# Two feed-forward layers of a fused float32 model: the high weight parts meet 512 activation columns instead of twice 256

## The reference, cut to what matters

```python
def swiglu(h, w_gu, w_down):
    g, u = jnp.split(h @ w_gu, 2, axis=-1)
    return (jax.nn.silu(g) * u) @ w_down
h = h + swiglu(rms_norm(h, f_norm[layer]), f_w_gu[layer], f_w_down[layer])
```

## Time and profile before

| | |
|---|---|
| Median of 3 runs | 966.72 us (965.94 to 967.09) |
| Span of the profiled execution | 967.0 us |
| Instructions | 19359, of them 7852 matmuls |
| TensorE matmul busy | 952.0 us, 98% |
| VectorE busy | 712.7 us, 74% |
| ScalarE busy | 489.3 us, 51% |
| GpSimd busy | 86.6 us, 9% |
| Mean DMA rate | 193 GB/s |

### The profile page before, as it was taken

One profiled execution on the slowest core, in us unless ns is written; L12 is line 12 of the kernel. 1 busy time (PEld: TensorE's weight loads), 2 busy tenths in 40 slices (PEclk: granted clock), 3 DMA queues, 4 the chain that ended last, 5 costly groups with the idle time before them and its releaser, 6 DMA issues.

```text
span 967.0 us, 19359 instructions
## 1 busy us (share of the span) xinstructions
PE 952.0 (98%) x7852; PEld 918.1 (95%) x7852; DVE 712.7 (74%) x1135; ACT 489.3 (51%) x717; POOL 86.6 (9%) x132
## 2 busy tenths in 40 slices
PE   8999999999999999899999999999999999999998
PEld 8999999999999888589999999999999999999998
DVE  5896877777759878968777777699876676565654
ACT  6344744433447547847344434447667555433441
POOL 6000000000000042420000000020000000000000
PEclk9999999999999999999999999999999999999999
DMA  8756768686845762037586868436344357564621
GB/s 273 264 175 220 259 197 294 232 295 197 289 149 163 238 218 88 1 132 261 182 291 227 293 221 286 152 105 199 99 166 159 109 170 259 176 218 133 234 67 44
DMA packets 129836, 186.99 MB, mean 193 GB/s; under 512 B 6384, under 2 KB 100976, under 8 KB 129776
## 3 DMA queue, kind: packets, MB, share of 16 engines
q1 hardware_dynamic: 122000, 159.69, 50.2%
q0 software_dynamic: 6912, 25.17, 7.4%
q10 hardware_dynamic: 864, 1.29, 0.4%
HBM read 185.09 MB, written 1.05 MB: 192 GB/s over the span
## 4 chain that ended last, share of the span: by engine, by line
PE 89%; DVE 4%; ACT 3%; DMA 2%; issue 1%; SPq 1%; DVEq 0%; ACTq 0%
PE ps L1909 46%; PE ps L1987 19%; PE ps L1905 13%; PE ps L1907 4%; DMA g_raw<-in_a_w_in 2%; ACT g_hi L679 1%; PE ps L2117 1%; PE ps L2064 1%; PE ps L2182 1%; PE ps L2197 1%; DVE g_lo L1186 0%; ACT opb_hi L697 0%; SPq L522 0%; ACT e_odd L893 0%; PE ps L2309 0%
## 5 line engine op out<-in xcount | busy, mean ns | idle before, releaser
L1909 PE MATMUL ps<-opa_hi,g_hi 128*128 128x256 f32 x864 | 228.7, 286 | 0.7 <-ACT g_hi L679 0.4
L1909 PE MATMUL ps<-opa_lo,g_hi 128*128 128x256 f32 x864 | 220.7, 283 | 0.0
L1909 PE MATMUL ps<-opa_hi,g_lo 128*128 128x256 f32 x864 | 181.4, 283 | 0.0
L1304 DVE TENSOR_TENSOR g_lo<-g_raw,g_hi 128x2048 fp32r<-128x2048 f32 x54 | 123.8, 2293 | 69.0 <-ACT g_hi L753 69.0
L1909 PEld LDWEIGHTS ps<-opa_hi,g_hi 128*128 128x128 f32 x864 | 165.4, 191 | 4.0 <-issue 2.9
L1909 PEld LDWEIGHTS ps<-opa_lo,g_hi 128*128 128x128 f32 x864 | 162.3, 192 | 0.1
L1987 PE MATMUL ps<-hid_hi,d_hi 128*128 128x256 f32 x528 | 147.6, 279 | 0.1
L1987 PE MATMUL ps<-hid_hi,d_lo 128*128 128x256 f32 x528 | 147.5, 279 | 0.0
L1987 PE MATMUL ps<-hid_lo,d_hi 128*128 128x256 f32 x528 | 147.3, 279 | 0.0
L1186 DVE TENSOR_TENSOR g_lo<-g_raw,g_hi 128x2048 fp32r<-128x2048 f32 x54 | 123.6, 2290 | 31.7 <-ACT g_hi L679 28.7
L1909 PEld LDWEIGHTS ps<-opa_hi,g_lo 128*128 128x128 f32 x864 | 138.7, 192 | 0.0
(11 more groups left out here) (339 smaller groups left out, 1811.0 us busy)
## 6 DMA issues: line engine op xcount, KB each, us to landing
g_raw<-in_f_w_gu SPq DMA_DIRECT2D x44, 1024.0 KB, 8.8
ada_raw<-in_w_ada POOLq DMA_DIRECT2D x48, 512.0 KB, 6.2
d_raw<-in_f_w_down SPq DMA_DIRECT2D x22, 1024.0 KB, 5.2
g_raw<-in_w_in SPq DMA_DIRECT2D x14, 1024.0 KB, 8.3
g_raw<-in_w_gate SPq DMA_DIRECT2D x11, 1024.0 KB, 7.3
g_raw<-in_w_up SPq DMA_DIRECT2D x11, 1024.0 KB, 9.8
d_raw<-in_w_down SPq DMA_DIRECT2D x11, 1024.0 KB, 5.2
g_raw<-in_a_w_in SPq DMA_DIRECT2D x8, 1024.0 KB, 7.6
```

The source lines that it names most:

```text
L1304: dve.tensor_tensor(part_view(g_lo, g0 + r, True), raw_cols(c % 2, r % 2, True), part_view(g_hi, g0 + r, True).bitcast(F32), ALU.subtract) ...
L1909: mm = pe.matmul(pair(b)[:, a, :], wt[:, a * P:(a + 1) * P], xt, **st)
```

## The change

The two activation buffers `opa_hi`, `opa_lo` become the two halves of one buffer `opa` of 512 columns, and so do `opb_hi`, `opb_lo`. In layers 0 and 1, from step g0+1 on, one matmul of 512 columns takes the place of the two that share the high weights. Its left 256 columns (high activations) fall where the low-weight product is added too, its right 256 columns (low activations) fall into the right half of the same bank; the two halves are added afterwards: ScalarE copies the right halves to `gu`, VectorE adds the left halves to them, and the multiplication by `rstd` now reads `gu`. A step has two whole banks, two pairs of banks in turn. Step g0 keeps matmuls of 256 columns but lays its sums out in the same way. In ScalarE's order the Silu moves behind `g_hi`; in VectorE's order the two operations of the side sum move apart, one behind the multiplication by `rstd`, one behind `g_lo`. Layer 2 keeps its code.

```diff
-    opa_hi = sb("opa_hi", [P, KT, T], F32R)
-    opa_lo = sb("opa_lo", [P, KT, T], F32R)
+    opa = sb("opa", [P, KT, 2 * T], F32R)
+    opa_hi, opa_lo = opa[:, :, 0:T], opa[:, :, T:2 * T]
...
+                if f < 2:
+                    act.wait_ge(g_done, s4 + (g0 + r + 1))
+                    if not first or d0 + r >= 2:
+                        act.wait_ge(hid_lo_made, s4 + (d0 + r - 1))
+                    act.activation(gu[:, r % 2, :, :], gate_and_up(r)[:, :, T:2 * T], ACT.Copy).then_inc(cross_copied, 1)
                 else:
+                    silu()
...
                     act.activation(part_view(g_hi, g0 + r, True), raw_cols(c % 2, r % 2, True),
                                    ACT.Copy).then_inc(g_hi_made, 1)
+                if f < 2:
+                    silu()
...
-                product = gate_and_up(r)[:, :, 0:T] if f == 2 else pair(gbank(g0 + r))
+                product = gate_and_up(r)[:, :, 0:T]
+                if f < 2:
+                    dve.wait_ge(cross_copied, s4 + (d0 + r + 1))
+                    dve.tensor_tensor(gu[:, r % 2, :, :], product, gu[:, r % 2, :, :], ALU.add).then_inc(gu_summed, 1)
+                    dve.wait_ge(gu_summed, s4 + (d0 + r + 1))
+                    product = gu[:, r % 2, :, :]
...
+        def opening_step(g, x, hi_ready, ready):
+            pe.wait_ge(g_hi_made, g + 1)
+            pe.wait_ge(g_lo_made, g + 1)
+            pe.wait_ge(g_evac, evacs(g - 3))
+            for k in range(KT):
+                hi_ready(k)
+                product(g, g_hi, x, k, HI_COLS, start=(k == 0))
+                product(g, g_lo, x, k, HI_COLS)
+            for k in range(KT):
+                ready(k)
+                mm = product(g, g_hi, x, k, LO_COLS)
+            mm.then_inc(g_done, 1)
+
+        def wide_step(g, x, n):
+            pe.wait_ge(g_hi_made, n)
+            pe.wait_ge(g_lo_made, n)
+            for k in range(KT):
+                product(g, g_hi, x, k, BOTH_COLS, start=(k == 0))
+                mm = product(g, g_lo, x, k, HI_COLS)
+            mm.then_inc(g_done, 1)
...
-            g_step(g0, hi, lo, ready, hi_ready=hi_ready)
             if f == 2:
+                g_step(g0, xin_hi, xin_lo, ready, hi_ready=hi_ready)
                 sum_squares(norm)
-            g_step(g0 + 1, hi, lo, no_wait, late_lo=True)
-            if f < 2:
+                g_step(g0 + 1, xin_hi, xin_lo, no_wait, late_lo=True)
+            else:
+                opening_step(g0, x, hi_ready, ready)
+                pe.wait_ge(g_evac, evacs(g0 - 1))
+                wide_step(g0 + 1, x, g0 + 2)
                 sum_squares(norm)
...
-                elif s is None or s >= 2:
-                    pe.wait_ge(hid_made, i * 4 + (d0 + r - 1))
+                    g_step(g0 + r + 2, xin_hi, xin_lo, no_wait, waited=True)
                 else:
-                    g_free(g0 + s + 2 - 4)
-                g_step(g0 + r + 2, hi, lo, no_wait, waited=True)
+                    pe.wait_ge(gu_summed, i * 4 + (d0 + r + 1))
+                    wide_step(g0 + r + 2, x, i * 4 + (g0 + r + 3))
                 d_step(i, r, s)
```

More of the change, by code:

```diff
@@ L203, in layer_kernel @@
     over_b = ExitStack()
-    opb_hi = sb("opb_hi", [P, KT, T], F32R, on=over_b)
-    opb_lo = sb("opb_lo", [P, KT, T], F32R, on=over_b)
+    opb = sb("opb", [P, KT, 2 * T], F32R, on=over_b)
+    opb_hi, opb_lo = opb[:, :, 0:T], opb[:, :, T:2 * T]
     d_raw = sb("d_raw", [P, 2, 2, D], on=over_b)
@@ L281, in layer_kernel @@
     c_copied = sem("c_copied")
+    cross_copied, gu_summed = sem("cross_copied"), sem("gu_summed")
     gu_made, gate_scaled, k_copied, r_turned = sem("gu_made"), sem("gate_scaled"), sem("k_copied"), sem("r_turned")
@@ L377, in gate_and_up @@
         return ps[:, 4 + 2 * (g % 2):6 + 2 * (g % 2), :]
+    HI_COLS, LO_COLS, BOTH_COLS = slice(0, T), slice(T, 2 * T), slice(0, 2 * T)
     def kv_tiles(s):
@@ L743, in step, with silu @@
                 g = gu[:, r % 2, 0, :]
-                act.wait_ge(gu_made, s4 + (d0 + r + 1))
+                def silu():
+                    act.wait_ge(gu_made, s4 + (d0 + r + 1))
+                    if f < 2:
+                        act.activation(g, g, ACT.Silu).then_inc(silu_made, 1)
+                    else:
+                        act.activation(g, g, ACT.Silu, bias=shift_cols(r % 2)[:, 0:1]).then_inc(silu_made, 1)
                 if f < 2:
-                    act.activation(g, g, ACT.Silu).then_inc(silu_made, 1)
+                    act.wait_ge(g_done, s4 + (g0 + r + 1))
+                    if not first or d0 + r >= 2:
+                        act.wait_ge(hid_lo_made, s4 + (d0 + r - 1))
+                    act.activation(gu[:, r % 2, :, :], gate_and_up(r)[:, :, T:2 * T], ACT.Copy).then_inc(cross_copied, 1)
                 else:
-                    act.activation(g, g, ACT.Silu, bias=shift_cols(r % 2)[:, 0:1]).then_inc(silu_made, 1)
+                    silu()
                 if not tail and not ahead:
@@ L1251, in split_d, with ada_pair @@
                               ALU.subtract).then_inc(d_lo_made, 1)
-        def ada_pair(f, i, q):
+        def ada_pair(f, i, q, parts=(0, 1)):
             m0 = 24 * f + q
-            dve.wait_ge(ada_loaded[q % 2], i * 32 + 16 * (m0 // 2 + 1))
             acc = ada_acc[:, bass.ds(i * 512 + 3072 * f, 512)]
-            for half in range(2):
+            for half in parts:
+                if half == 0:
+                    dve.wait_ge(ada_loaded[q % 2], i * 32 + 16 * (m0 // 2 + 1))
                 k, raw = 2 * q + half, ada_raw[:, q % 2, half, :]
@@ L1290, in step @@
                     dve.tensor_copy(shift_cols(r % 2).unsqueeze(2), gate_and_up(r)[:, :, T:T + 1])
-                product = gate_and_up(r)[:, :, 0:T] if f == 2 else pair(gbank(g0 + r))
+                product = gate_and_up(r)[:, :, 0:T]
[4 more added lines that the diff above has]
+                    product = gu[:, r % 2, :, :]
                 dve.tensor_tensor(gu[:, r % 2, :, :], product,
                                   rstd[:, :].unsqueeze(1).to_broadcast([P, 2, T]), ALU.mult).then_inc(gu_made, 1)
+                with_ada = f < 2 and not tail and not ahead
+                if with_ada:
+                    ada_pair(f, i, r, (0,))
                 dve.wait_ge(gu_made, s4 + (d0 + r + 1))
@@ L1305, in step @@
                                       part_view(g_hi, g0 + r, True).bitcast(F32), ALU.subtract).then_inc(g_lo_made, 1)
+                if with_ada:
+                    ada_pair(f, i, r, (1,))
                 dve.wait_ge(hid_hi_made, s4 + (d0 + r + 1))
@@ L1317, in step @@
                     split_g(g0 + 3)
-                if f < 2:
-                    if not tail and not ahead:
-                        ada_pair(f, i, r)
             split_g(g0 + 2)
@@ L1911, in g_step, with product @@
                 mm.then_inc(g_done, 1)
+        def product(g, parts, x, k, cols, start=False):
+            for a in range(2):
+                mm = pe.matmul(gate_and_up(g)[:, a, cols], parts[:, g % 2, k, a * P:(a + 1) * P], x[:, k, cols],
+                               start=start, stop=(k == KT - 1), skip_group_check=True)
+            return mm
+        def opening_step(g, x, hi_ready, ready):
[17 more added lines that the diff above has]
+            mm.then_inc(g_done, 1)
         def g_free(g):
@@ L1916, in g_free @@
                 if first <= g < first + FT:
-                    pe.wait_ge(hid_made, FT * f + g - first + 1)
+                    pe.wait_ge(gu_summed, FT * (f + 1))
                     return
@@ L2053, in _ @@
         if last_stage >= 2:
-            ffn(0, 1, opa_hi, opa_lo, a_filled("n1"), a_hi_filled("n1"))
+            ffn(0, 1, opa, a_filled("n1"), a_hi_filled("n1"))
         if last_stage >= 3:
```

12 lines of the change are left out of this document (6 added, 6 removed).

## The result

The changed kernel takes 974.36 us (median of 4 runs, 973.45 to 976.26), the kernel before 966.33 us in the same comparison. The ratio is 1.0083, with a 95% interval of 1.0069 to 1.0098: **8.0 us slower**. Forecast were 971.9 us, in a range of 962 to 981.

A forecast was written before the change was run, and what follows sets the result against it. TensorE, with matmuls under way for 98% of the span, was taken as the bound. Terms +10.2 (waits), +3.0 (clock), +0.6 (layer ends), -0.6 (given back), -8.0 (wide matmuls) gave +5.2: 966.7 to 971.9 us, range 962 to 981.

The forecast's parts named there:

- The large term: Start of layers 0 and 1: g0+2 reuses g0's banks and waits for step 0's addition; 5.1 us lost in each.
- The 1.6 us ahead of g0+1: Step g0+1 now waits for g_lo at its start, beginning 1.60 us later in layer 0; counted inside g0+2's loss.
- the clock: Behind the idle wait in each of layers 0 and 1, a granted-clock drop costing 1.5 us each, 3.0 lost.
- the clock holds: Rival: no clock drop in the new waits at the layer starts; +2.2 us, 968.9; chance 0.08.
- the cover: Steady state: the added ScalarE copy (0.59 us) and VectorE addition (0.69) stay hidden beside 8.3 us of TensorE; cost nothing.
- The end of a layer: Last down steps: hidden features come 1.3 us later against the step's end; 0.3 us lost each, 0.6 in all.
- what was given back: Step g0+3's old wait for its g_lo goes, since g0+2 starts later; 0.3 us each, 0.6 gained.
- 13.3 + 11.7 = 25.0 ns for a pair of matmuls in each layer: Gain from wide matmuls behind the start, 20 wide steps a layer with 16 each: 8.0 us gained.
- 0.223 to 0.227: Expected sign: microseconds from a wide matmul's start to the next start, with narrow ones at 0.118 to 0.120.
- the 0.216 that was to speak against the forecast: Sign against: a wide matmul's distance of 0.216 us, or of 0.24, would make the forecast wrong.
- the overhead goes with the columns: Rival: a 512-column matmul costs two of 256, no gain, 980.3 us; chance 0.15 together with the chip splitting it.
- the difference carries over: Whole kernel: the profiled span, 967.0, lies 0.3 us above the median 966.7, so the sum was added to the median.

The follow-up runs named there:

- two passes: Changed kernel with step g0+1 running its 16 high-weight wide matmuls first, then waiting for g_lo, then 16 low-weight ones: 973.18 us.
- The two cut kernels: Each 512-column matmul issued as two of 256: in the changed kernel, 980.15 us; in one with reordered layer starts that remove the waits, 967.41 us.
- the filler above: Changed kernel plus 18 float32 matmuls of 128 columns, results unread, issued while TensorE would wait for the first sum in layers 0 and 1: 974.77 us.

## Why the prediction was right, and where not

**Right: slower, and why.** The large term was the wait of g0+2 for the first addition. Forecast were 4.3 to 4.5 us from the squares to the next matmul; both layers have 4.27. Moving that addition and its copy, and nothing else, brought 7.2 us back. The 1.6 us ahead of g0+1 are there (1.49 us idle) and go with two passes.

**Right: the clock.** The rival "the clock holds" is out. At both holes the clock was at 0.50 for 3.4 us, worth 2.9 us (forecast 3.0), and with the hole closed the clock stayed (mean 1.000). The forecast took the length of the drop from one example, though, 3.4 us at 0.51, in which fifteen matmuls took 3.20 us, 1.4 us behind the end of an idle stretch of 2.13 us, and in one hole each of two later kernels it was twice that, 6.8 us.

**Right: the cover.** TensorE is idle nowhere in the steady state. VectorE waits 1.4 to 1.5 us a step for ScalarE's copy, as in these rows of its timeline in the middle of layer 0, so the addition has room:

```profile
210.94 0.69 DVE L1311 TENSOR_TENSOR gu<-ps,gu 128x512 f32<-128x512 f32 x1 [1.53 <-ACT gu L760]
...
219.25 0.69 DVE L1311 TENSOR_TENSOR gu<-ps,gu 128x512 f32<-128x512 f32 x1 [1.37 <-ACT gu L760]
```

The end of a layer (0.6 forecast, 0.5 found) and what was given back (0.6 and 0.8) were sized well.

**Wrong: the price of the wide matmul.** The term that was mis-sized is the gain of "13.3 + 11.7 = 25.0 ns for a pair of matmuls in each layer", one overhead for each matmul that goes. No run shows it: it is 0.120 and 0.1185 us less 0.107, the author's estimate of bare streaming. It gave 8.0 us; the profile has 4.5. Per pair of matmuls that became one, a step got shorter by (5.753 - 5.586)/16 = 10.4 ns in layer 0 and (5.685 - 5.622)/16 = 3.9 ns in layer 1 (unrounded step lengths), not by 13.3 and 11.7. The two cut kernels put nearly all of it down to the width, in both layers. A wide matmul takes 0.233 us in both, not 0.223 to 0.227, and no run has one at the 0.216 that was to speak against the forecast (the shortest, with two bytes read of each four, took 0.226). In layer 0 that is 6.5 ns less than two of 256 columns in the cut kernel (119.8 each), and the narrow matmuls that stay got 3.9 ns cheaper too (116.0), which the forecast did not have. In layer 1 it is 3.4 ns less than two (118.3 each), and the narrow ones stay at 118.2.

Above bare streaming, estimated as half of the distances at the granted clock of 0.50, stand 9.3 ns in layer 0 and 11.5 in layer 1 for 256 columns, and 19.8 and 19.9 for 512. So most of the excess grows with the columns, where the forecast had it stay the same from 256 to 512. That none of it is there at the lower clock is supposed in the estimate and not shown. The rival "the overhead goes with the columns" comes nearest to the price of the wide matmul, in layer 1 above all, but its outcome, no gain at all, did not come, and its cause, a limit of what is read from SBUF in a time, was supposed; no run shows it.

Why the gain is larger in layer 0 is not shown. The shift by 64 bytes shows that 256-column matmuls pay there for where buffers lie: 0.30 us a step, of which the wide matmuls saved 0.17. That the two are the same cost is argued only, since no kernel has both the width and the shift. The difference of 1.5 ns between the layers stood in the rows, and the prediction took it as each layer's "overhead" without asking what differs between them.

**Wrong, without effect: the span against the median.** The prediction said that the profiled span lies 0.3 us above the median and "the difference carries over". Each later run lists its time beside its span, and 1.7 to 1.9 us always lie outside it (974.63 and 972.9 for the changed kernel). A span of 967.0 therefore belongs to a run of nearly 969, some 2 us above the typical one, and the row with the reason was there, the chance drop at 338 us. None of the terms rested on it, so the sum added to the median was not touched; whoever compares the two profiled spans alone is misled by 2 us.

In all, the terms were 8.6 - 5.2 = 3.4 us too low, 3.5 of it the wide matmuls. The medians differ by 8.0, so 0.6 us of the account are not placed. Of this, 0.4 lies between the 8.6 and the 8.2 by which the two profiled executions would differ without chance.

## What to carry to other kernels

When a change makes a buffer's release depend on another engine, look at the first use behind a boundary, not at the steady state: there the releasing operation may stand behind a chain (root, `g_hi`, copy) that never mattered. Put the one operation that frees the buffer ahead of that chain. Price a wider instruction by a run with it cut in two, and read the step in every stage that has it; a median that comes out as expected does not show that its parts did. Where two stages with the same instructions run at different speeds, ask what differs (here where a buffer lies) before giving a cause to the difference.

## What the runs showed of the hardware that was not expected

- At half the granted clock matmuls took less than twice the time: 256 columns 116.0 ns in layer 0 and 118.2 in layer 1 at 1.00, 213 at 0.50; 512 columns 233.1 and 233.2 at 1.00, 427 at 0.50. Reading two bytes of each four, of weights and activations both, lowered the times at 1.00 to 114 and 226 ns; overwriting instead of adding in PSUM did not lower them (0.46 us for two wide, 0.24 for two narrow).
- The place of buffers decides it in part: a shift of 64 bytes a partition, of `opa` and all that is declared behind it, took a 256-column matmul from 0.120 to 0.1134 us in layer 0, from 0.1184 to 0.1168 in layer 1, and the kernel from 966.8 to 955.2 us in one run; a shift of `opa` by 8 KB did nothing.
- One plain float32 matmul of 128 columns leaves two records of 0.11 us: 18 of them are the 36 in the row of the filler above, 119.58 - 115.65 = 3.93 us for all. The 0.109 us of the expectation for 34 of them is therefore met by a record, and a matmul takes 0.22.
- The lower clock (0.50) lasted 3.4 us at both holes of the changed kernel and 6.8 at two of later ones (layer 0 with the late low weights, 116.6 to 123.4; layer 1 with two bytes read, 456.6 to 463.4). An idle stretch of 2.1 us at 336 us was followed by a drop in one execution, one of 1.7 us in another was not.
